# An embedding stage whose first five loads are issued in the stage before it

## What is computed

```python
def rms_norm(x, g):
    y = xf * lax.rsqrt(jnp.mean(xf * xf, axis=-1, keepdims=True) + EPS)
    return (y * g)
...
    # one layer, 512 tokens x 1024
    n = rms_norm(h, norm_mix_g); z, xbc, dt, q, k, v = split(n @ w_in)
    h = h + concat(ssd_mixer(...), diff_attention(...)) @ w_out
    h = h + peer_ffn(rms_norm(h, norm_ffn_g), wq, sub_k1, sub_k2, expert_u, expert_v)
    # per head the 16 best of 128 x 128 experts:
    #   act = gelu(xt . u[eidx]); w = act * softmax(top); out = sum(w * v[eidx])
    e = rms_norm(p @ ple_proj, ple_norm_g)                       # p is 512 x 256
    gate = sigmoid(rms_norm(h, ple_gate_norm_g) @ ple_gate_w)    # 1024 x 1024
    h = h + gate * e
```

## Time and profile before

| what | us |
|---|---|
| median of 3 runs | 1787.14 |
| lowest, highest | 1783.83, 1787.2 |
| the profiled execution, its own time | 1788.47 |
| its span, first to last instruction | 1786.7 |
| PE busy | 1674.8 (94%) |
| GpSimd busy | 1076.0 (60%) |

### The profile page before, as it was taken

One profiled execution on the slowest core, in us unless ns is written; L12 is line 12 of the kernel. 1 busy time (PEld: TensorE's weight loads), 2 busy tenths in 40 slices (PEclk: granted clock), 3 DMA queues, 4 the chain that ended last, 5 costly groups with the idle time before them and its releaser, 6 DMA issues. The chain is left out here.

```text
span 1786.7 us, 26267 instructions
## 1 busy us (share of the span) xinstructions
PE 1674.8 (94%) x9133; PEld 1494.9 (84%) x9133; DVE 1196.8 (67%) x2525; ACT 603.6 (34%) x862; POOL 1076.0 (60%) x542
## 2 busy tenths in 40 slices
PE   6998999869989989799999999979999999999978
PEld 5797855867789989799999999968888888888848
DVE  6576464440097989895999999156676767766645
ACT  2122333111122332235556565332333333333241
POOL 4552200235336867586666666569898988988622
PEclk9998955989999999999999999989999999999989
DMA  4121000132036878686899999889999999999631
GB/s 187 71 95 48 24 24 1 48 133 95 24 125 205 298 261 271 213 288 221 314 342 354 343 339 338 292 318 359 355 354 368 357 360 352 357 365 355 220 141 48
DMA packets 169835, 413.63 MB, mean 232 GB/s; under 512 B 12832, under 2 KB 95392, under 8 KB 164512
## 3 DMA queue, kind: packets, MB, share of 16 engines
q1 hardware_dynamic: 131168, 253.33, 40.2%
q0 software_dynamic: 36864, 134.23, 21.6%
q10 hardware_dynamic: 1728, 25.17, 3.6%
HBM read 358.15 MB, written 54.53 MB: 231 GB/s over the span
## 5 line engine op out<-in xcount | busy, mean ns | idle before, releaser
L1045 POOL TENSOR_TENSOR s_lo<-s_raw,s_hi 128x1024 fp32r<-128x1024 f32 x224 | 537.8, 2402 | 220.4 <-ACT s_hi L1159 216.8
L1090 PE MATMUL s_psum<-hn_hi,s_hi 128*128 128x384 f32 x1024 | 350.6, 342 | 28.4 <-POOL s_lo L1045 28.4
L1159 ACT CAST s_hi<-s_raw 128x1024 fp32r<-128x1024 f32 x256 | 267.0, 1047 | 250.4 <-PE s_psum L1136 150.8
L1090 PE MATMUL s_psum<-hn_lo,s_hi 128*128 128x384 f32 x1024 | 345.2, 337 | 0.0
L1090 PE MATMUL s_psum<-hn_hi,s_lo 128*128 128x384 f32 x1024 | 345.1, 337 | 0.0
L1136 PE MATMUL s_psum<-s_hi,s_whi 128*128 128x512 f32 x768 | 300.1, 391 | 11.1 <-DVE s_wlo L1391 11.0
L1136 PE MATMUL s_psum<-s_lo,s_whi 128*128 128x512 f32 x768 | 299.8, 390 | 0.0
L1136 PE MATMUL s_psum<-s_hi,s_wlo 128*128 128x512 f32 x768 | 299.7, 390 | 0.0
L1079 POOL DMA_INDIRECT s_gtile<-in_v_t,s_v_row x128 | 221.0, 1727 | 25.0 <-issue 24.3
L1090 PEld LDWEIGHTS s_psum<-hn_hi,s_hi 128*128 128x128 f32 x1024 | 195.0, 190 | 31.3 <-POOL s_lo L1045 31.1
L1090 PEld LDWEIGHTS s_psum<-hn_lo,s_hi 128*128 128x128 f32 x1024 | 194.9, 190 | 0.0
(11 more groups left out here) (297 smaller groups left out, 2918.4 us busy)
## 6 DMA issues: line engine op xcount, KB each, us to landing
s_raw<-in_u_t SPq DMA_DIRECT2D x128, 512.0 KB, 4.9
s_raw<-in_v_t SPq DMA_DIRECT2D x128, 512.0 KB, 7.3
act_scratch<-s_acts SPq DMA_DIRECT2D x128, 192.0 KB, 4.3
gate_scratch<-s_gtile ACTq DMA_DIRECT2D x12, 2048.0 KB, 10.2
scores<-act_scratch SPq DMA_DIRECT2D x32, 768.0 KB, 7.3
scores<-gate_scratch SPq DMA_DIRECT2D x32, 768.0 KB, 10.9
m_w_raw<-in_w_in SPq DMA_DIRECT2D x12, 1024.0 KB, 4.8
r_w_raw<-in_w_q SPq DMA_DIRECT2D x8, 1024.0 KB, 4.8
```

Of the source, the lines that this page charges most:

```text
L1045: pool.tensor_tensor(lo[:, s, :], raw[:, s, :], hi[:, s, :].bitcast(F32), ALU.subtract).then_inc(lo_ready[s], 1)
L1090: last = pe.matmul(psU[:, s % 2, :], uu[:, s, d * P:(d + 1) * P], hh[:, d, P:T], start=(n == 0 and d == 0), stop=(n == 2 and d == DC - 1))
L1159: act.copy(hi[:, s, :], raw[:, s, :]).then_inc(hi_ready[s], 1)
```

## The change

A class `Ahead` holds four tensors (W_ple, p, the gain, and the two places of raw gate weights) at fixed addresses from the place on where `hn_hi` and `hn_lo` lie, 8 x 4 KB per partition in all, and five semaphores that are allocated ahead of retrieval. `Ahead.load` issues five loads: p, W_ple, gate blocks 0 and 1, and the gain. The experts stage's SP stream calls it behind its last group of v tiles. The embedding stage uses these tensors and semaphores, keeps their space reserved, and its SP stream starts with gate block 2. Behind the last stage the five semaphores are cleared, with a barrier of their own.

```diff
+class Ahead:
+    def __init__(self, nc, offset):
+        at = lambda name, shape, dst: nc.alloc_sbuf_tensor_at(name, shape, F32, offset=offset + 4 * D * dst)
+        self.wp = at("x_wp", [P, PLE // P, D], 0)
+        self.pin = at("x_p", [P, TB, PLE], 2)
+        self.gain = at("x_gain", [P, D], 3)
+        self.w_raw = at("x_w_raw", [P, 2, DC, Weights.WIDTH], 4)
+        self.sems = Semaphores(nc)
+        self.p_loaded, self.wp_loaded, self.gain_loaded = (self.sems("x_" + n) for n in ("p_loaded", "wp_loaded", "gain_loaded"))
+        self.w_loaded = [self.sems(f"x_w_loaded{i}") for i in range(2)]
+    def load(self, sp, io):
+        sp.dma_start(self.pin[:, :, :], io["p"].rearrange("(t p) d -> p t d", p=P)).then_inc(self.p_loaded, 16)
+        sp.dma_start(self.wp[:, :, :], io["w_ple"].rearrange("p (c n) -> p c n", c=PLE // P)).then_inc(self.wp_loaded, 16)
+        for n in range(2):
+            sp.dma_start(self.w_raw[:, n, :, :], io["w_gate"][n].rearrange("p (c n) -> p c n", c=DC)).then_inc(self.w_loaded[n], 16)
+        sp.dma_start(self.gain[:, :], io["ple_gain"]).then_inc(self.gain_loaded, 16)
...
 # experts, SP's stream, behind the loop over the groups
+            ahead.load(sp, io)
...
 # embedding
-        weights = Weights(sb, new_sem, "e", 4)
-        wp = sb("e_wp", [P, PC, D])
-        pin = sb("e_p", [P, TB, PLE])
+        sb("e_ahead", [P, 8 * D])
+        weights = Weights(sb, new_sem, "e", 4, ahead.w_raw, ahead.w_loaded)
+        wp, pin, gain = ahead.wp, ahead.pin, ahead.gain
...
-            sp.dma_start(pin[:, :, :], io["p"].rearrange("(t p) d -> p t d", p=P)).then_inc(sem["p_loaded"], 16)
-            sp.dma_start(wp[:, :, :], io["w_ple"].rearrange("p (c n) -> p c n", c=PC)).then_inc(sem["wp_loaded"], 16)
-            sp.dma_start(gain[:, :], io["ple_gain"]).then_inc(sem["g_loaded"], 16)
-            for n in range(4):
+            for n in range(2, 4):
                 weights.load(sp, n, io["w_gate"][n])
...
 # block_kernel
         mixer(nc, shared, io)
+        ahead = Ahead(nc, nc.sbuf_base)
...
-        embedding(nc, shared, io, out)
+        embedding(nc, shared, io, out, ahead)
+        ahead.sems.free()
```

More of the change, by code:

```diff
@@ L122, with __init__ @@
     WIDTH = 256
-    def __init__(self, sb, new_sem, tag, count):
+    def __init__(self, sb, new_sem, tag, count, raw=None, loaded=None):
         self.count = count
-        self.raw = sb(f"{tag}_w_raw", [P, 2, DC, self.WIDTH])
+        self.raw = sb(f"{tag}_w_raw", [P, 2, DC, self.WIDTH]) if raw is None else raw
         self.hi = sb(f"{tag}_w_hi", [P, 2, DC, self.WIDTH], F32R)
@@ L130, in __init__ @@
             [new_sem(f"{tag}_w_{n}{i}") for i in range(2)] for n in ("loaded", "hi_ready", "lo_ready", "used"))
+        if loaded:
+            self.loaded = loaded
     def load(self, sp, n, src):
@@ L889, in retrieval, with experts @@
     new_sem.free()
-def experts(nc, shared, io, act_dram, gate_dram, h_dram):
+def experts(nc, shared, io, act_dram, gate_dram, h_dram, ahead):
     con, hn_hi, hn_lo, scores, h = (shared[k] for k in ("con", "hn_hi", "hn_lo", "scores", "h"))
@@ L1451, in experts, with embedding @@
     new_sem.free()
-def embedding(nc, shared, io, out):
+def embedding(nc, shared, io, out, ahead):
     h, con, cols = (shared[k] for k in ("h", "con", "cols"))
@@ L1460, in embedding @@
         sb = lambda n, s, d=F32: ctx.enter_context(nc.sbuf_tensor(n, s, d))
-        names = ["p_loaded", "g_loaded", "pT_ready", "e_ready", "e_scaled", "sumsq_ready", "ms_ready", "root_ready", "xn_ready",
-                 "high_ready", "nT_ready", "gate_ready", "added", "stored", "pe_tile", "act_line", "dve_line", "wp_loaded"]
+        names = ["pT_ready", "e_ready", "e_scaled", "sumsq_ready", "ms_ready", "root_ready", "xn_ready",
+                 "high_ready", "nT_ready", "gate_ready", "added", "stored", "pe_tile", "act_line", "dve_line"]
         sem = {n: new_sem("e_" + n) for n in names}
@@ L1478, in embedding @@
         nT = (nT_hi, nT_lo)
-        gain = sb("e_gain", [P, D])
         gate = sb("e_gate", [P, 4 * TB, 256])
@@ L1505, in _ @@
         def _(pe):
-            pe.wait_ge(sem["p_loaded"], 16)
+            pe.wait_ge(ahead.p_loaded, 16)
             for c in range(PC):
@@ L1512, in _ @@
             pe.wait_ge(sem["pT_ready"], PC)
-            pe.wait_ge(sem["wp_loaded"], 16)
+            pe.wait_ge(ahead.wp_loaded, 16)
             for i in range(2 * TB):
@@ L1580, in _ @@
             step(dve.reciprocal(st[:, 7, 4:8], st[:, 6, 0:TB]))
-            dve.wait_ge(sem["g_loaded"], 16)
+            dve.wait_ge(ahead.gain_loaded, 16)
             for t in range(TB):
@@ L1606, in block_kernel @@
             retrieval(nc, shared, io, h_dram)
-            experts(nc, shared, io, act_dram, gate_dram, h_dram)
-        embedding(nc, shared, io, out)
+            experts(nc, shared, io, act_dram, gate_dram, h_dram, ahead)
+        embedding(nc, shared, io, out, ahead)
+        ahead.sems.free()
 def constants():
```

## The result

The changed kernel takes **1791.04 us** (median of 15 runs, 1788.23 to 1792.61); the kernel before takes 1786.23 in the 15 runs timed beside it (1783.83 to 1788.91). The ratio is 1.0026, with a 95% interval of 1.0018 to 1.0034, so +4.8 us (3.2 to 6.1). The forecast was 1792.7, +5.6.

A forecast was written before the change was run, and what follows sets the result against it. The prediction took the embedding stage's start as the bound, headed by a 4.08 us wait for p's load. On 1787.14 us it added 5.15 (blocked sums), 0 (clock) and 0.45 (end): 1792.7 us, range 1786.5 to 1795.5.

The forecast's parts named there:

- What is late after the load: Embedding start: without p's load wait, ScalarE's root holds the copies next, so products start only 1.8 us earlier.
- What comes with the loads: Embedding start: GpSimd's freed gate cuts alternate with VectorE's sums and block them, products start 5.15 us later.
- The clock: Embedding products: PE's share at the lower 1.2 GHz stays 3.8 us, effect 0, bounds -1.9 to +1.3 us.
- The gathers: End of the values loop: gathers sharing the DMA engines with the early loads have 5.3 us of cover, cost 0.
- The end: Behind the last stage: one more semaphore clearing and barrier, +0.45 us, bounds 0.3 and 0.6.
- The sum: Whole kernel: 5.15 + 0 + 0.45 = +5.6 us on 1787.14, giving 1792.7 us; chance 0.48.
- The chance of 0.62: Whole kernel: probability given to a measured time slower than before by more than about 0.2%, 3.6 us.
- Rival 1: Embedding start: VectorE's first sum starts before GpSimd's cut, products +3.45 us, 1791.0 us in all; chance 0.25.
- Rival 2: Embedding start: only VectorE's small 128x4 instruction is blocked, not the sums; products +1.25 us, 1788.8 us; chance 0.11.
- Rival 3: Embedding start: GpSimd doesn't get in before VectorE's small instruction ends, load's gain stays; 1785.8 us, down to 1783.9; chance 0.13.
- Rival 4: Values loop's end: early loads delay gathers beyond their 5.3 us of cover; 2 us past it gives 1794.7; chance 0.03.

The follow-up runs named there:

- e1_gate_late: Changed kernel with only p, W_ple and the gain loaded early, all four gate blocks loaded in the embedding stage; 1783.76 us, ratio to before 0.9994.
- e2_cuts_wait: Changed kernel, all five loads early, with GpSimd's cuts waiting for VectorE's small mean of squares; 1783.97 us, ratio to before 0.9992.
- e9_cut_03us: Changed kernel with a 256-column GpSimd memset ahead of its first cut; one run, 1788.32 us to 1783.97 before.
- e10_cut_07us: Changed kernel with a 768-column GpSimd memset ahead of its first cut; one run, 1790.82 us to 1783.97 before.
- e4_one_clear: Changed kernel with the early semaphores cleared together with the embedding stage's, without the extra clearing and barrier; 1789.38 us, ratio to before 1.0023.
- e3_gate_only: Changed kernel with only the two gate blocks loaded early, p, W_ple and the gain at the embedding's start; 1790.32 us, ratio to before 1.0034.
- e8_loads_ahead: Changed kernel with GpSimd's cuts waiting for VectorE's mean and the five loads issued ahead of the last four v tiles; 1789.45 us, ratio to before 1.0030.
- e7: Changed kernel with only ScalarE's two copies of p's transpose moved ahead of its squares; 1782.46 us, ratio to before 0.9984.
- e5_cut_at_1us: Changed kernel with GpSimd's first cut held until PE has transposed p's first half; one run, 1782.95 us to 1785.1 before.

## Why the prediction was right

**What is late after the load: right.** It said that ScalarE's root, and not PE's transposes, comes next, and that p's load is worth 1.8 us. e1_gate_late and e2_cuts_wait give 2.02. The term was small by 0.2: the two copies take 1.06 together and start under the root's end, where the sum laid 1.21 behind it.

**What comes with the loads: right, and it is the change's whole cost.** The steps, as forecast and as measured in the changed kernel: 1.90 for the first L167 and 1.90; first sum's end 1.09 after it and 1.07; L169 4.48 beyond that sum and 4.36; second sum's end 1.09 and 1.08 later; the small one at the next cut's end +0.02 and +0.03. (For its 1.09 the prediction gives no source; the traces bear it out.) The custom operation, which no row of before showed beside a cut, is blocked like L1588. By the rule of the Trainium skill cited in the prediction ("SBUF — State Buffer", section "SBUF: two separate sides") it had to be, as it reads two inputs in SBUF; its mean of 4.2 us agrees. The same sentence limits this to GpSimd operations that read SBUF. That agrees too: VectorE's first sum keeps its 1.23 us beside GpSimd's MEMSET, which reads nothing and runs for 0.31 us in e9_cut_03us and for 0.74 in e10_cut_07us. The products' start moved by +4.73 (6.75 to 11.47) for the +5.15 of the sum. Of the 0.42 between them L169 and the second L167 make 0.13 and 0.11, the root's issue close behind the small instruction 0.07, and the copies, which start under the root's end, 0.13; GpSimd's start 0.03 after S works the other way.

**The clock: 0 in this trace, but partly by luck.** The stretch at 0.50 grew from 10.2 to 17.1 us, but ended 3.7 us into the products instead of 3.8. PE had stopped at 1695.95, fell to 1.2 GHz at 1698.9, and rose only after 3.7 us of products; the 1.94 us of transposes in between did not bring it back. That it is 0 belongs to this one execution. In e4_one_clear the products also start 11.47 in, and 6.0 us of them are slow: +1.1 us against before, near the +1.3 that the prediction gave as the upper bound. What the term is on average over the runs, no run shows.

**The gathers: right at 0.** VectorE's idle time ahead of the six last adds:

```profile
1695.99 3.68 DVE L1474 TENSOR_TENSOR h<-h,s_psum 128x512 f32<-128x512 f32 x6 [3.52 <-PE s_psum L1160]
```

It was 5.30, and PE still ends last. How much of the cover the loads took isn't shown: in the eight kernels that issue all five loads in this place the idle time is 2.64 to 4.57, and with the two gate blocks alone (e3_gate_only) it is 6.70, more than before. That e8_loads_ahead has only 0.99 left, and loses, is through the v tiles and not through the gathers.

**The end: right.** 0.45 was taken, 0.4 measured: 3.39 against 3.02 us from the last add to the span's end, and 3.01 with the second clearing taken out (e4_one_clear).

**The sum.** 4.73 + 0.4 = 5.1; the span's end moved by 88.49 - 83.50 = 4.99 against S, and the medians by 4.81. The forecast's +5.6 is 0.8 above, of which 0.4 is the products' start and 0.4 lies within the scatter. In microseconds the forecast, 1792.7, lies 1.7 above the measured 1791.04; the other 0.9 is its base, the median of 3 runs given then, 1787.14 for 1786.23. The chance of 0.62 went to slower by more than 0.2%: the ratio of 1.0026 is above that, but its interval reaches down to 1.0018.

**The rivals.** Rival 1 (1791.0) is nearest to the measured time by chance: the trace has GpSimd first, by 0.03 us, and the median cannot tell the two cases 1.7 us apart. All four profiled executions in which nothing holds the first cut back (changed, e3, e4, e7) have GpSimd first by 0.03 us; how the other runs went isn't known. Rival 2 falls with the 2.94 and 5.50 of the sums. Rival 3, that GpSimd does not get in, holds for e1 and e2, whose edits see to it: 0.9994 and 0.9992, which on the base of 1785.88 is -1.1 and -1.4 us, where rival 3 had -1.35. Their intervals reach 1, so the medians alone don't tell it from no change; the products' start, 2.02 us earlier, does. Rival 4 stayed away, with 3.5 us to spare in the changed kernel's trace and 2.6 in the closest of its kind (e5_cut_at_1us).

## What to carry to other kernels

Before a load is moved ahead, list who waits for it, and what each of them will then run beside: a GpSimd that is set free at a bad moment can cost more than the load's wait was worth, and one wait on it takes that loss away (6.1 us here). And look at what stands behind a late instruction only by its engine's order; moving the two copies ahead of the root made the same 7.6 us of blocking free. Where the wait that goes (4.08 us here) is longer than the next engine's slack, only the slack's part of it (2.0 us) is gained.

## What the runs showed of the hardware

- The sharing between VectorE and GpSimd is by turns, and not by engine: a GpSimd cut that has waited 0.5 us or longer gets in between two VectorE instructions that would follow back to back (e9 and e10: the second takes 2.90 us), and one issued 0.01 us ahead of the second does not (e5: 1.22).
- What is blocked ends a fixed time after its blocker: 1.07 to 1.08 us for the sum over 1024 columns, 0.02 to 0.03 for the 128x4 instruction, which went from 0.17 to 1.74 and 4.33 us. A length in a profile that counts from issue thus shows mostly the neighbour's length.
- Not every small VectorE instruction is caught. The RECIPROCAL on the same 128x4 kept 0.18 us in the changed kernel, issued at 1711.40 while GpSimd's L169 of 1711.11 to 1715.61 ran:

```profile
1711.40 0.18 DVE L1589 RECIPROCAL e_st<-e_st 128x4 f32<-128x4 f32 x1 [0.34 <-ACT e_st L1557]
1711.61 4.55 DVE L1591 TENSOR_SCALAR e_xn<-h,e_st 128x1024 f32<-128x1024 f32 x1
```

  The TENSOR_SCALAR right behind it waited for that L169 to its end.
- Issuing a DMA can hold SP up: the issue of p's load took 5.18 us in e8_loads_ahead and 0.39 in the changed kernel. Why isn't shown. The DMA engines were 0.93 busy in the one case and, from 1667.9 to 1668.4, 0.85 in the other.
- Two executions whose products start at the same place can differ by 1.1 us in them (15.83 in the changed kernel, 16.97 in e4_one_clear), by when the granted clock goes from 0.50 to 1.00: 3.7 us into them and 6.0.
